# Retrieval stage of a hybrid layer on one core: four instead of two units left out of the dense product, and dots carried on while block 1's weight matrix is built from stacked tokens

## The reference, cut to what matters

```python
q = (tb @ w_query).reshape(tbn, PEER_HEADS, PEER_KEY_DIM)      # 8 heads
s1, s2 = ...                                                   # 128 + 128 key scores
v1, i1 = lax.top_k(s1, 16); v2, i2 = lax.top_k(s2, 16)
top_s, pos = lax.top_k(cand, 16)                               # of 16 x 16 sums
idx = jnp.take_along_axis(cand_idx, pos, axis=-1)              # i1 * 128 + i2
gate = jax.nn.softmax(top_s)
u = expert_u[idx]; v = expert_v[idx]                           # tables of 16384 x 2048
act = jax.nn.gelu(jnp.einsum('td,thkd->thk', tb, u))
return jnp.einsum('thk,thkd->td', gate * act, v)
```

## Time and profile before

| | |
|---|---|
| median of 3 runs | 1875.18 us (1873.02 to 1877.64) |
| profiled execution | 1877.48 us, of which the span from first to last instruction is 1875.7 us |
| busy share | PE 79%, DVE 71%, POOL 47%, ACT 23% |
| bytes | 666.96 MB, 356 GB/s over the span; 486.58 MB on POOL's queue |
| mean granted TensorE clock | 0.862 |

### The profile page before, as it was taken

The page is one execution under the profiler, slowest core; times in us unless marked ns, Lnnn a source line. Parts: engine busy times, 40 slices in busy tenths (PEclk is TensorE's granted clock), DMA queues, the critical chain, the costliest instruction groups (busy, mean ns, idle before and its releaser), DMA issues.

```text
span 1875.7 us, 13800 instructions
## 1 busy us (share of the span) xinstructions
PE 1477.3 (79%) x4521; PEld 733.0 (39%) x4521; DVE 1322.4 (71%) x1813; ACT 431.1 (23%) x1158; POOL 881.7 (47%) x666
## 2 busy tenths in 40 slices
PE   6989999999999455655565655555499999999995
PEld 3434564565459311211111223333374444434442
DVE  3137887776138989888989988788875665655667
ACT  3011211120122222112212366655470100000000
POOL 0012243311005788878888877656315555533331
PEclk9999999999999766665666577777699999999998
DMA  9998988886658999999999998989539999999997
GB/s 364 361 364 312 343 337 319 310 323 220 221 191 338 373 419 419 419 419 418 419 418 419 419 418 334 355 339 353 187 119 382 414 413 413 413 415 413 415 414 282
DMA packets 164022, 666.96 MB, mean 356 GB/s; under 512 B 16432, under 2 KB 19056, under 8 KB 124784
## 3 DMA queue, kind: packets, MB, share of 16 engines
q0 software_dynamic: 92160, 486.58, 65.2%
q1 hardware_dynamic: 71360, 176.36, 24.9%
q10 hardware_dynamic: 432, 3.15, 0.4%
HBM read 661.74 MB, written 4.29 MB: 355 GB/s over the span
## 4 chain that ended last, share of the span: by engine, by line
PE 30%; DMA 25%; DVE 22%; POOL 13%; issue 6%; ACT 3%; SPq 1%; DVEq 0%; POOLq 0%; ACTq 0%
DMA arena<-in_expert_v,arena 18%; POOL arena L556 13%; DVE arena L1330 9%; PE PS L1763 6%; PE PS L1622 6%; PE PS L1523 5%; DMA arena<-in_expert_u,arena 5%; PE PS L1866 3%; DVE arena L1372 3%; PE PS L1504 3%; PE PS L1839 2%; PE PS L1479 1%; DVE arena L1377 1%; DMA arena<-in_w_in 1%; DVE arena L1342 1%
## 5 line engine op out<-in xcount | busy, mean ns | idle before, releaser
L1330 DVE CUSTOM_DVE_ANT_0 arena<-arena 128x2048 f32<-128x2048 f32 x256 | 578.5, 2289 | 82.1 <-DMA arena<-in_expert_u,arena 80.7
L1839 PE MATMUL PS<-arena 128*128 128x512 f32 x512 | 375.7, 878 | 206.2 <-DMA arena<-in_expert_v,arena 201.5
L556 POOL DMA_INDIRECT arena<-in_expert_v,arena x256 | 366.0, 1430 | 351.4 <-DVE arena L1372 134.1
L556 POOL DMA_INDIRECT arena<-in_expert_u,arena x256 | 418.5, 1635 | 235.4 <-DVE arena L1305 90.4
L1872 PE MATMUL PS<-arena 128*128 128x512 f32 x1024 | 441.2, 593 | 6.2 <-DMA arena<-in_expert_v 6.2
L1872 PEld LDWEIGHTS PS<-arena 128*128 128x128 f32 x1024 | 194.5, 190 | 252.8 <-issue 240.4
L1839 PEld LDWEIGHTS PS<-arena 128*128 128x128 f32 x512 | 124.0, 267 | 415.6 <-DMA arena<-in_expert_v,arena 311.4
L1372 DVE SCALAR_TENSOR_TENSOR arena<-arena 128x1024 f32<-128x1024 f32 x95 | 122.1, 1285 | 105.5 <-DMA arena<-in_expert_v,arena 103.8
L1047 DVE SCALAR_TENSOR_TENSOR arena<-arena 128x1024 f32<-128x1024 f32 x120 | 160.8, 1340 | 23.8 <-DMA arena<-in_w_mod 20.8
L906 ACT ACTIVATE arena<-arena 128x4 f32<-128x4 f32 x64 | 13.1, 205 | 707.8 <-DVE arena L1330 676.1
L1866 PE MATMUL PS<-arena 128*128 128x128 f32 (+1 forms) x512 | 84.9, 324 | 114.3 <-ACT arena L893 112.3
(11 more groups left out here) (236 smaller groups left out, 1328.5 us busy)
## 6 DMA issues: line engine op xcount, KB each, us to landing
arena<-in_w_mod POOLq DMA_DIRECT2D x128, 512.0 KB, 6.9
arena<-in_expert_v SPq DMA_DIRECT2D x128, 512.0 KB, 7.9
arena<-in_w_mod SPq DMA_DIRECT2D x32, 1024.0 KB, 14.3
arena<-in_w_in SPq DMA_DIRECT2D x28, 1024.0 KB, 14.7
arena<-in_w_out SPq DMA_DIRECT2D x16, 1024.0 KB, 12.6
arena<-in_w_query SPq DMA_DIRECT2D x8, 1024.0 KB, 8.5
arena<-in_x SPq DMA_DIRECT2D x4, 1024.0 KB, 6.1
arena<-cum_rows SPq DMA_DIRECT2D x4, 1024.0 KB, 9.4
```

Source lines behind the costliest of these rows:

```text
L556: nc.gpsimd.indirect_dma_start(slot, None, table, bass.IndirectOffsetOnAxis(ap=rows[:, n:n + 1], axis=0),).then_inc(arrived, 16)
L1330: V.tensor_tensor_reduce(out=rows, in0=rows, in1=h2row[u // PH], scale=1.0, scalar=0.0, op0=ALU.mult, op1=ALU.add, accum_out=dots[:, u % B ...
L1839: ins = M(PS[:, b, :], diag_slot[m % DIAGS], vslot[m % V_SLOTS][:, b * NQ:(b + 1) * NQ], start=(m == 0), stop=(m == BLK - 1))
```

## The change

- `DENSE` goes from 14 to 12 units. Slots 192 to 255 are now gathered as full rows for v, so block 1 has 64 slots in the dense product (`LEFT`) instead of 96.
- `G[1]` is built in 16 batches instead of 32: because a token has only 64 slots in it, tokens t and t+64 are stacked in the upper and lower 64 partitions. The expert numbers and coefficients are written twice side by side before the transpose (`indices_twice`, `coef_twice_out`). DVE makes the second halves, ACT the first halves, PE uses 64 partitions per product.
- Beside those 16 batches DVE works off dots 192 to 208, one ahead of each batch; their rows and 16 half rows for PE come through the ring ("pe" items), which is 5 slots wide for its first 20 items.
- Expert rows of block 0 keep their rate until dot 130 (62 rows) and then stand denser, 50 rows within 57 dots. Block 0's batches stand beside dots 130 to 197, one in every 1.75. `oh1` has 4 buffers instead of 2, `oh2` 5 instead of 4, the diagonals 6 instead of 5 and are made 10 dots ahead instead of 6.
- Units are routed every 12.25 dots instead of every 16. The copy of the scores is dropped, and the two halves of the expert number are selected together (three operations of 512 elements instead of six of 256).
- The ring holds then 32 pairs with 32 u-rows, 12 u-rows, and 64 full rows. `close(0)` is moved in ahead of the last 15 full rows, the addition of the dense right half ahead of the last 7, and the last row is added in halves.

```diff
-DENSE = UNITS - 2
+DENSE = UNITS - 4
 N_DENSE = DENSE * TOPK
+LEFT = N_DENSE - BLK
+STACKED = BATCHES // 2
-DIAGS = 5
+DIAGS = 6
-V_AT = {n: [m for m in range(V_EARLY) if 20 + 203 * m // V_EARLY == n] for n in range(N_DENSE)}
-H_AT, OH_AT, G_AT, OUT_AT = [{n + 2 * b: b for b in range(BATCHES)} for n in (146, 150, 153, 154)]
-ITEMS = [x for i in range(2 * TOPK) for x in (("u", N_DENSE + i), ("pair", BLK + 2 * i))]
-ITEMS += [x for i in range(TOPK) for x in (("full", N_DENSE + 2 * i), ("full", N_DENSE + 2 * i + 1), ("pair", BLK + 4 * TOPK + 2 * i))]
-N_RING = 4
+V_POS = [20 + 110 * m // 62 if m < 62 else 130 + 57 * (m - 62) // 50 for m in range(V_EARLY)]
+OH2_AT, OH1_AT, OUT_AT, G_AT = [{n + 7 * b // 4: b for b in range(BATCHES)} for n in (130, 133, 137, 143)]
+ROUTE_AT = {16 + 49 * (r - 2) // 4: r for r in range(2, UNITS)}
+ITEMS = [x for i in range(8) for x in (("u", N_DENSE + 2 * i), ("u", N_DENSE + 2 * i + 1), ("pe", V_EARLY + 2 * i))]
+ITEMS += [("u", N_DENSE + 16 + i) for i in range(4)]
+ITEMS += [x for i in range(LEFT // 2) for x in (("pair", BLK + 2 * i), ("u", N_DENSE + 20 + i))]
+ITEMS += [("u", N_DENSE + 20 + LEFT // 2 + i) for i in range(44 - LEFT // 2)]
+ITEMS += [("full", N_DENSE + i) for i in range(4 * TOPK)]
+WIDE_ITEMS = 20
+RING_OF = [k % 5 if k < WIDE_ITEMS else (k - WIDE_ITEMS) % 4 for k in range(len(ITEMS))]
+GAIN_AT, CLOSE_AT, RIGHT_AT = 132, len(ITEMS) - 16, len(ITEMS) - 8
...
+            def first_halves_stacked(b):
+                act.wait_ge(slots_evac, 4)
+                act.wait_ge(g_ps, BATCHES - 3 + b if b < 4 else BATCHES + 2 * (b - 3))
+                o, t = oh1[b % 4], b * BATCH
+                for i in range(BATCH):
+                    ins = A(o[:, i, :], iota128, ACT.Abs, scale=-1.0, bias=eT[:, 0, t + i:t + i + 1])
+                step(ins)
+                A(o, o, ACT.Relu, scale=-1.0, bias=1.0).then_inc(oh1_ready, 1)
...
+            for b in range(STACKED):
+                g_out(BATCHES + 2 * b)
+                g_out(BATCHES + 2 * b + 1)
+                if b + 3 < STACKED:
+                    first_halves_stacked(b + 3)
+                if V_EARLY + 2 + b < BLK:
+                    diagonal(V_EARLY + 2 + b)
...
-                go(V.tensor_copy(s_cur, scores[u // PH][:, u % PH, :]))
...
+            def second_halves_stacked(b):
+                if b == 0:
+                    dve.wait_ge(slots_evac, 6)
+                dve.wait_ge(g_ps, BATCHES + (2 * (b - 4) if b >= 5 else 0))
+                t = b * BATCH
                 for i in range(BATCH):
+                    ins = ts(oh2[b % 5][:, i, :], iota128, eT[:, 1, t + i:t + i + 1], coefT[:, t + i:t + i + 1],
                              ALU.is_equal, ALU.mult)
                 ins.then_inc(oh2_dve, 1)
...
-            for b in range(BATCHES, 2 * BATCHES):
-                first_halves(b)
-                if b not in ACT_BATCHES:
-                    second_halves(b)
             for k in range(len(ITEMS)):
                 item(k)
+                kind, n = ITEMS[k]
+                if kind == "u" and 0 <= n - N_DENSE - 1 < STACKED:
+                    second_halves_stacked(n - N_DENSE - 1)
...
+            def scatter_stacked(b):
+                pe.wait_ge(oh1_ready, BATCHES + b + 1)
+                pe.wait_ge(oh2_dve, b + 1)
+                for h in range(2):
+                    bank_free(BATCHES + 2 * b + h)
+                    part = slice(h * LEFT, (h + 1) * LEFT)
+                    for i in range(BATCH):
+                        ins = M(PS[:, 6 + h, i * P:(i + 1) * P], oh1[b % 4][part, i, :], oh2[b % 5][part, i, :], start=True, stop=True)
+                    ins.then_inc(g_ps, 1)
...
-            coef_transpose(1)
-            for b in range(BATCHES):
-                scatter(BATCHES + b)
+            coef_transpose_stacked()
+            for b in range(STACKED):
+                scatter_stacked(b)
                 if b % 2:
-                    expert_rows(V_EARLY + b // 2)
+                    row_pair(V_EARLY + b - 1)
```

More of the change, by code:

```diff
@@ L44 @@
 U_EARLY = 20
-BUF = 4
+BUF = 6
 PARTS = 4
@@ L123, in ring_count @@
 def ring_count(k):
-    return 16 * U_EARLY // EARLY + sum(32 if kind == "pair" else 16 for kind, _ in ITEMS[k % N_RING:k + 1:N_RING])
+    mine = [j for j in range(k + 1) if RING_OF[j] == RING_OF[k]]
+    return 16 * U_EARLY // EARLY + sum(32 if ITEMS[j][0] in ("pe", "pair") else 16 for j in mine)
 def build(nc, x, ctx_in, w_mod, w_in, w_fmix, w_out, w_query, k1t, k2t, expert_u, expert_v,
@@ L614, in _ @@
                     gather_v(m)
[L615 to L621, removed]
+            for k in range(len(ITEMS)):
                 item_load(k)
@@ L874, in second_halves, with slots_out @@
-            def second_halves(b):
[L876 to L881, removed]
+            def slots_out():
+                act.wait_ge(slots_ps, 1)
+                A(eT[:, 0, :], PS[:, 2, 0:P], ACT.Copy)
+                A(eT[:, 1, :], PS[:, 2, P:2 * P], ACT.Copy).then_inc(slots_evac, 1)
@@ new lines, in coef_out, with indices_twice, stacked @@
+            def coef_out():
+                act.wait_ge(slots_ps, 2)
+                A(coefT, PS[:, 3, 0:P], ACT.Copy).then_inc(slots_evac, 1)
+            def indices_twice():
+                act.wait_ge(idx_ready, DENSE)
+                for a in range(2):
+                    ins = A(e_twice[:, a], e_all[:, a, BLK:N_DENSE].unsqueeze(1).to_broadcast([P, 2, LEFT]), ACT.Copy)
+                ins.then_inc(slots_evac, 1)
+            def stacked(dst, src):
+                A(dst[0:LEFT, 0:P // 2], src[0:LEFT, 0:P // 2], ACT.Copy)
+                return A(dst[LEFT:P, 0:P // 2], src[LEFT:P, P // 2:P], ACT.Copy)
@@ L911, in unit @@
                     act.wait_ge(coef_done, u * TOPK + GR * (g + 1))
-                    if g == 1 and 1 <= u < UNITS - 1:
-                        softmax_exp(u + 1)
                     first = u * TOPK + GR * g
-                    for n in range(first, first + GR):
-                        for m in V_AT.get(n + 6, []):
-                            diagonal(m)
[L918 to L923, removed]
+                    group = range(first, first + GR)
@@ L929, in _ @@
             for u in range(DENSE):
                 unit(u)
-            coef_out(1)
-            for m in range(V_EARLY, V_EARLY + V_SLOTS):
-                diagonal(m)
-            second_halves(ACT_BATCHES[0])
-            for b in range(BATCHES, 2 * BATCHES):
[L936 to L940, removed]
+            first_halves_stacked(0)
@@ L964, in _ @@
             for h in range(2):
-                act.wait_ge(right_added, h + 1)
-                part = slice(HALF + h * NQ, HALF + (h + 1) * NQ)
-                A(squares[3][:, h * NQ:(h + 1) * NQ], acc[:, part], ACT.Square, accum_out=fsq[:, 5 + h:6 + h]).then_inc(fsq_ready, 1)
+                act.wait_ge(row_added, len(ROWS) + h)
+                square(1 + 2 * h, acc[:, h * HALF:(h + 1) * HALF], 4 + h)
             last_root(1)
@@ L1863, in scatter @@
-                pe.wait_ge(g_evac, b - 1) if b >= 2 else pe.wait_ge(sc_evac, UNITS)
-                used = slice(0, SLOTS[b // BATCHES])
+                pe.wait_ge(oh2_ready, b + 1)
+                bank_free(b)
                 for i in range(BATCH):
-                    ins = M(PS[:, 6 + b % 2, i * P:(i + 1) * P], oh1[b % 2][used, i, :], oh2[b % 4][used, i, :], start=True, stop=True)
+                    ins = M(PS[:, 6 + b % 2, i * P:(i + 1) * P], oh1[b % 4][:, i, :], oh2[b % 5][:, i, :], start=True, stop=True)
```

272 lines of the change are left out of this document (147 added, 125 removed).

## The result

The change made the kernel slower: 1886.02 us median (15 runs, 1875.61 to 1902.06) against 1876.99 us (15 runs, 1868.9 to 1880.55) before. The ratio is 1.0054, with a 95% interval of 1.0032 to 1.0076, so it is 0.3 to 0.8% slower, where 1.9% faster was forecast. The profiled execution has a span of 1883.5 us.

What follows compares the result with a forecast made beforehand. The kernel was taken as DMA-bound with a 94 us hole, then PE and DMA both full. Dot 192 at 1227 us, build to 1302, last row 1830 and an 11 us end gave span 1841, median about 1840; range 1818 to 1872.

Steps and rivals of the forecast that it cites:

- Bytes: 32 slots move from the dense product to full rows: 16.8 MB more, 40 us at 419 GB/s.
- Steps 1 and 2: Dots before the build: dot 130 at 1000 us, then 3.75 us a dot to 186, dot 192 at 1227.
- The rival that the tie stays: Block 0's batches lose DMA time as before, 4.40 us a dot, +37 us, 1877; chance 0.06, half of it 0.12.
- One of the signs of being wrong: Dots before the build: the DMA under 400 GB/s between 1000 and 1227 us.
- Step 3: Block 1's build: 8 us of lead-in, then 16 batches at 4.2 us, 67 us, done at 1302 us.
- paced by the ring: Build: "pe" slots come free late and following dots wait a round trip; 5.5 us a batch, +21 us, 1861; chance 0.15.
- Its other half: Build, same rival of chance 0.15: changes of tile height cost PE 1.9 us a batch; 5.5 us a batch, 1861.
- The low clock: Build: PE falls to 1.2 GHz; wholly at it 7.3 us a batch, +50 us, 1890; chance 0.07.
- Step 4: After the build: 217 MB at 414 GB/s take 524 us; with `close(0)` costing 4 us, last row at 1830.
- Two of the signs named for being wrong: A build over 90 us, and a full-row phase at the end under 400 GB/s.
- Step 5: Kernel's end: 11 us for half additions, square, sums, gain, outputs and last store; end at 1841 us.

Runs made afterwards that it cites:

- rows_even: Against the changed kernel: all 128 expert rows of block 0 stand beside the dots, evenly from dot 20 to 186, none in the build; 1850.25 us.

## Why the prediction was wrong

Span forecast 1841, measured 1883.5. Of the 42.5 us 34 lie in one term, the build, 7 in the stages behind it and 1.5 ahead of it.

- **Bytes**: right. 683.72 - 666.96 = 16.8 MB more.
- **Steps 1 and 2**, dots to 192: right in time. Dot 130 at 999.3 us (1000), dots 130 to 186 took 217 us (214), 187 to 191 12.1 (13), dot 192 at 1228.5 (1227). The looser tie of PE to ACT did what was said: PE waited 4.0 us for `g_out` in 1000 to 1225 us, where it had waited 101. The rival that the tie stays is refuted. One of the signs of being wrong came all the same, by a hair: 399 GB/s between 1000 and 1227 us, where under 400 was named. The 3.75 us a dot of the forecast are themselves only 402 GB/s, so that sign was set too near to say anything.
- **Step 3, the build, failed**: 109.2 us against 75, 34 us of the error. Its start was nearly right (first scatter 9.7 us after dot 192, 8 forecast); the rest is 99.5 us for 16 batches, 6.2 each against 4.2. The step took the largest of four resources and then let the ring move 5 MB in each 14.4 us. It counted slots and not what has to happen before a slot comes free. A pair's slot is freed by the last link of PE's list, which itself needs a dot loaded later through the same ring, and POOL's order makes every later gather wait as well. The rival "paced by the ring" named this place, and priced it at 5.5 us a batch without walking the loop; the walk, with the rows that were there (a row product 1.9 to 3.6 us, a scatter 2, a dot 2.2, a second half 1.1), needed only one landing time more. Even so it was too cheap by 13 us, about what the low clock added to the loop (some 15 us by the estimate above). Its other half, a cost of changing tile height, no run shows.
- **The low clock**, the rival on the slower side, was half right. The clock did fall (0.74), and no term of step 3 had it: its 3.65 us a batch for PE were fast-level rows. But by the same estimate the loop would have kept the build near 94 us without it, and **rows_even**, without the loop, took 59.8 us at 0.51.
- **Step 4**: 545.8 us from the first dense product to the end against 539. The dense stage ran at 412 GB/s as forecast (414) and PE ended ahead of the rows, though its product took 467 us and not 439; the rows set the end, so that cost nothing. Mis-sized was the stage behind it: 374 GB/s instead of 414 over 67.8 us, 6.5 us. POOL refills four slots while DVE works at 2.35 us a row, and a fifth slot gave 390. Two of the signs named for being wrong came clearly: a build over 90 us and a phase of full rows under 400 GB/s.
- **Step 5**: 10.7 us from the last row's landing to the end against 11.
- **The Trainium skill's two warnings.** The first of the Trainium skill (TensorEngine Tiling (Array Packing), Key Properties) is that a change of tiling mode drains TensorE. Products on 64 partitions right behind full-height rows took 1.71 us for 16 at the fast clock, less than the 1.95 of the 96-partition ones, and the next row product started as they ended (1253.10 us above), so no drain is to be seen. The second of the Trainium skill (SBUF — State Buffer, SBUF: two separate sides) is that GpSimd cannot write descriptors while VectorE runs an fp32 two-port operation. Nine of POOL's gathers in the build of **rows_even** ran beside VectorE's second halves and took 0.94 us, as with VectorE idle, so no sign of that either, as forecast. Beside a dot it is otherwise; see the last section.

Why slower than before at all, in DMA time against 419 GB/s: the bytes cost 40 us. The stage of dots loses 229.9 x (1 - 399/419) = 11 us instead of the 36 + 11 up to the old build, 36 gained. The new build loses 109.2 x (1 - 238/419) = 47 us, as many as the old one's 46. The stages behind it lose 8 + 7 against 11, 4 more; the end is 7 shorter. 40 - 36 + 1 + 4 - 7 = 2 us of the spans' 7.8. The other 6 are 2.5 MB: by these rates 335.6 MB went over in the windows instead of 333.1. Some 2 MB of them the old kernel moved outside its windows, 1 MB more than the new one before 998.6 us (349 GB/s against 348) and 1 MB more in its last 17.7 us (119 GB/s, against 98 in the new one's last 10.7); at three digits a rate this is not sure to better than 1 MB. So the expected gain did not go anywhere behind the build: it was never made, since the work put into the hole lengthened the hole.

## What to carry to other kernels

When slots of one ring are freed by two engines, walk one turn of the loop before counting slots: from the issue behind a freed slot, over landing and use, to the instruction that frees the next; if that instruction stands in its engine's list behind work that needs a later slot, the turn's length is the pace, however few bytes are moved. Consume such a slot at the earliest place that its data allow. Price the loop's own products at the low clock if they stand behind a wait like the 4 us here; outside a loop the low clock may cost nothing. And a stage in which all engines are half idle is to be read for such a loop first: here one exchange of two calls was worth 29 us, 26 of them in the build, and moving the rows out altogether 36.

## What the runs showed of the hardware that was not expected

A gather of 1.049 MB was used 5.6 to 7.8 us after its issue in the loop, by a dot that had waited for it, against a median of 14.4 us from issue to landing over the kernel before. So a row comes in about half the time where the DMA is half empty, and the stage still moves only 238 GB/s, because POOL issues too few. Scatter halves on 64 partitions ran 16 in 1.71 us at the fast clock and 3.06 at the slow one, without a stall where the height changed.

POOL's gathers are held up by some of DVE's instructions and not by others. First from the build of the changed kernel, a gather that begins while a dot runs, then from **rows_even** one that begins while the second halves run:

```profile
1284.38 2.29 DVE L1373 CUSTOM_DVE_ANT_0 arena<-arena 128x2048 f32<-128x2048 f32 x1 [2.40 <-DMA arena<-in_expert_u,arena]
1284.56 2.92 POOL L566 DMA_INDIRECT arena<-in_expert_u,arena  x1 [0.30 <-issue]
```

```profile
1262.30 1.33 DVE L1395 TENSOR_SCALAR arena<-arena 128x128 f32<-128x128 f32 x4
1262.65 0.94 POOL L566 DMA_INDIRECT arena<-in_expert_u,arena  x1 [2.32 <-DVE arena L1371]
```

The first ends 0.81 us behind the dot. In the whole trace of the changed kernel 213 gathers began within a dot: their median is 2.19 us, and the median end lies 0.81 us behind the dot's. The 21 that began while a full row was added (line 1416) took 2.29 us, and end 0.81 us behind it too. The 217 that began with DVE idle took 0.94 us, and so did 15 that began within a `MATCH_REPLACE8` of the routing. The dots and the additions read two tensors; no run here tests whether that is the reason. In the loop it cost little, as DVE was mostly idle when POOL issued.
